# A two-block transformer kernel: how the first norm's scales arrive, who clears the queries, how many projection pieces run ahead of the first scores, and four zero products fewer ahead of attention 2

## The chip, the cores and the metric

The kernel runs on one core of one Trainium2 chip. The metric is the device time of one execution in microseconds; the figure of a kernel is the median of several runs.

## The reference, cut to what matters

The kernel computes two transformer blocks in float32 over 256 tokens of width 1024. Only the first steps of block 1 and the entry of block 2 matter here.

```
# block 1
h    = x * rsqrt(mean(x*x) + 1e-6) * attn_pre_g             # (256, 1024)
proj = h @ w_in                                             # (1024, 2304)
q_a, k_a, v_a, q_b, k_b, v_b = split(proj)                  # 512, 128, 128, 512, 512, 512
y_a  = sliding window attention with sinks (8 heads), then RMS norm
y_b  = differential attention (4 heads, two maps each), then RMS norm per head
x    = x + rms_norm(concat(y_a, y_b) @ w_out, attn_post_g)
x    = x + rms_norm(conv_ffn(rms_norm(x, ffn_pre_g)), ffn_post_g)
# block 2: adaptive norm of x by c, w_in_2, stick-breaking and dilated attention, w_out_2,
# then 32 experts with two-level routing; every expert's weights are read
```

## The kernel before, in words

TensorE (PE) multiplies, ScalarE (ACT) and VectorE (DVE) prepare operands and empty its banks, GpSimd (POOL) builds constants and takes inverse roots, SyncE (SP) issues the weight loads. Each engine runs its own list in written order and waits on semaphores; the order around the change is written out by hand.

**Weights and products.** Weights come in chunks of 2 MB into a ring of three places (chunk 0 in two halves). Most products are made of three: ACT rounds a half chunk to a short float (`split_one`, L1529), DVE subtracts to get the rest (`split_one`, L1871), and PE multiplies high by high, high by rest, rest by high (`product`, L903 to L905). The activations are split likewise: ACT's `rounded` (L1515) and DVE's `low` (L1852) read the turned tiles from the banks and scale them by a column of gains.

**Head of the kernel.** ACT issues 12 small loads into `stage` (rows of 128 values: taps of the convolution, c, and eight gain vectors, `attn_pre_g` among them) and then loads its table. SP issues x (two halves of 512 KB), the weight chunks, `swa_sinks` and the four lambda rows. DVE first clears the query tile `qz` (L2068, 128 x 4096), then takes the mean squares of both token tiles (L1818), POOL the roots (L783), and DVE scales both tiles (L2073). PE meanwhile makes 16 products of zeros (`stay_awake`, L874), turns token tile 0 (L892), makes four more products of zeros, waits for all 12 small loads, turns `stage` in three pieces (L1085 to L1087) and turns token tile 1. DVE copies the turned gains to `vec` (L2076 to L2078), and only then do ACT's `rounded`, DVE's first `split_one` and PE's first products (`project_first(4)`, L1103, L1110, L1125) go.

**Pieces.** The projection of block 1 is cut into 16 pieces (`items1`): 0 to 3 are queries of chunk 0; 4 (a key) and 5 (a value, 48 short products) are of chunk 1; 6 is a query of chunk 1; 7, 9, 10 and 11 are of chunk 2, 8 of chunk 1, 12 to 14 of chunk 3, 15 of chunk 4. A key or query piece is 24 products. `AHEAD = [6, 10]`: pieces 0 to 5 are made before attention 1, each in its own bank; the others are made between the units of attention (`BETWEEN`, L464). ACT empties even pieces, DVE odd ones (`take`).

**Attention 1** (L968) has 12 units. In step i PE makes scores i+1 (L978), turns the probabilities of unit i-1 (L1002), makes the value products of unit i-2 (L1016), and then the pieces of `BETWEEN[0][i]`. `scores(0)` waits until pieces 0 to 5 are taken. DVE's list ahead of its first softmax is: lambda, take pieces 1 and 3, split both halves of chunk 2, take piece 5, wait for the masks (`bias`, L816 and L818 on POOL).

**Ahead of attention 2** (L1228 to L1242) PE turns token tile 0 of the normed rows, sums the modulation's columns, turns the sums, makes five products of zeros (L1236), turns token tile 1, makes three more, and starts the products of the second projection.

**The experts** (from L1458) take 16 pairs; SP loads each matrix (2 MB) into one of ten places as soon as PE has read what lay in it (`pair_loads`, L679).

Of the kernel before, what the change touches and what calls it, by code (L numbers as in the profile page):

```python
# [19 lines left out]
def two_block_kernel(nc, a, out):  # L20
# [4 lines left out]
    ALU = mybir.AluOpType  # L25
# [5 lines left out]
    P = 128  # L31
# [3 lines left out]
    KD = D // P  # L35
# [40 lines left out]
    N_IN = 0  # L76
# [15 lines left out]
    with ctx:  # L92
# [11 lines left out]
        def sem(name):  # L104
            return ctx.enter_context(nc.semaphore(name))
# [3 lines left out]
        kT = sb("kT", [P, 8, S])  # L109
# [61 lines left out]
        hsq = cell(T, DIFF_H)  # L171
        frac = cell(NEXP)


# [78 lines left out]
        stage = kT[:, 0:2, :].rearrange("p k s -> p (k s)")[:, 0:384].rearrange("p (a b) -> p a b", a=3)  # L253

        PS = [ctx.enter_context(nc.psum_tensor(f"bank{i}", [P, HALF], f32)) for i in range(8)]

# [10 lines left out]
        s_rows = sem("s_rows")  # L267
        s_sink = sem("s_sink")
        s_lamv = sem("s_lamv")
# [184 lines left out]
        def item_waits(blk, n):  # L454
# [8 lines left out]
        AWAKE_AFTER = [{10: 2}, {}]  # L463
        BETWEEN = [{0: [6], 1: [7], 2: [8], 3: [9], 4: [10], 5: [11], 6: [12], 7: [13, 14], 8: [15]},  # L464
                   {0: [10, 11], 1: [12], 2: [13], 3: [14], 4: [15, 16], 5: [17], 6: [18], 7: [19]}]
# [134 lines left out]
        def _(sp):  # L600
# [29 lines left out]
            for c in range(1, LANES):  # L630
                straight(N_IN + c, w_in[:, :, c * HALF:(c + 1) * HALF])
            sp.dma_start(sinks, a["swa_sinks"][0].partition_broadcast(P)).then_inc(s_sink, 16)
            for n, name in enumerate(("diff_lq1", "diff_lk1", "diff_lq2", "diff_lk2")):
# [127 lines left out]
        def _(pool):  # L761
# [34 lines left out]
            pool.memset(ones[:, :], 1.0).then_inc(s_const, 1)  # L796
            pool.memset(zrow[:, :], 0.0).then_inc(s_const, 1)
            inverse_roots(T)
            then(pool.memset(from_here[:, :], 1.0))
# [70 lines left out]
        def _(pe):  # L870
            def stay_awake(bank, count):

                for _ in range(count):
                    pe.matmul(bank[:, :], zrow[:, 0:P], zrow[:, :], start=True, stop=True)  # L874
# [204 lines left out]
            pe.wait_ge(s_const, 3)  # L1079
            stay_awake(PS[7], 16)  # L1080
            turn("attn1", hn, range(T - 1))

            stay_awake(PS[6], 4)
            pe.wait_ge(s_stage, 16 * 12)
            pe.transpose(PS[7][:, 0:P], stage[:, 0, :], ident[:, :])  # L1085
            pe.transpose(PS[7][:, P:2 * P], stage[:, 1, :], ident[:, :])
            pe.transpose(PS[7][:, 2 * P:2 * P + 53], stage[0:53, 2, :], ident[0:53, 0:53]).then_inc(s_vecT, 1)  # L1087
            turn("attn1", hn, range(T - 1, T))
            pe.wait_ge(s_vec, 1)

            def project_first(count):
# [31 lines left out]
                for n in range(count):  # L1123
# [3 lines left out]
                    last.then_inc(s_gemm[0], 1)  # L1127

            project_first(4)
            for n in range(4, AHEAD[0]):  # L1130
                project(0, N_IN, n)
# [102 lines left out]
            for n in range(2):  # L1234
                turn_column_sums(n)
            stay_awake(PS[6], 5)  # L1236
            turn("attn2", rows2, range(T - 1, T))
# [240 lines left out]
        def _(sc):  # L1478
# [8 lines left out]
            cw = a["conv_w"].rearrange("o j (f p) -> (o j f) p", p=P)  # L1487
            cb = a["conv_b"].rearrange("o (f p) -> (o f) p", p=P)
            sc.dma_start(stage[:, 0, :], cw[0:P, :]).then_inc(s_stage, 16)
            sc.dma_start(stage[0:FT, 1, :], cw[P:P + FT, :]).then_inc(s_stage, 16)  # L1490
# [131 lines left out]
            sc.wait_ge(s_vec, 1)  # L1622
            rounded("attn1", lambda k: vec[:, 2, R_PRE + k:R_PRE + k + 1])
            split_one(N_IN, 1)
# [3 lines left out]
            sc.activation(lam2, lam2, ACT.Exp).then_inc(s_lame, 1)  # L1628
            take(0, range(AHEAD[0]))
            softmaxes(0, BETWEEN[0], SPLITS[0])  # L1630
# [159 lines left out]
        def _(ve):  # L1790
# [276 lines left out]

            ve.memset(qz[:, :, :], 0.0).then_inc(s_qzero, 1)  # L2068
            for t in range(T):
# [5 lines left out]
            ve.wait_ge(s_vecT, 1)  # L2075
            ve.tensor_copy(vec[:, 0:2, :], PS[7][:, 0:2 * P].rearrange("p (a b) -> p a b", a=2))  # L2076
            then(ve.tensor_copy(vec[:, 2, 0:53], PS[7][:, 2 * P:2 * P + 53]))
            ve.tensor_scalar(subc, vec[:, 2, R_SUB:R_SUB + 1], 1.0 - LAMBDA_INIT, None, ALU.mult).then_inc(s_vec, 1)  # L2078
            split_one(N_IN, 0)
            low("attn1", lambda k: vec[:, 2, R_PRE + k:R_PRE + k + 1])  # L2080
            split_one(N_IN, 1)
            split(N_IN + 1)

            ve.wait_ge(s_lamv, 64)
# [4 lines left out]
            ve.wait_ge(s_sink, 16)  # L2089
# [371 lines left out]
```

## Time and profile before

| | us |
|---|---|
| median of 3 runs | 1016.91 |
| the three runs | 1016.75, 1016.91, 1019.25 |
| the profiled execution's own time | 1018.49 |
| its span | 1016.8 |

The span runs from the first to the last instruction of the profiled execution; its own time holds 1.7 us more around it. Times in the profile are microseconds from the span's start. Busy time is counted per engine; "idle before" is how long an engine sat idle before an instruction, with what released it. The granted clock is 1.00 at 2.4 GHz and 0.50 at 1.2 GHz.

### The profile page before, as it was taken

Reading aid. Unit: us, or ns where it says so; the run is one execution under the profiler, and the core shown is the slowest. Engines: PE = TensorE matmul, PEld = TensorE weight load, DVE = VectorE, ACT = ScalarE, POOL = GpSimd, SP = SyncE. Lnnn points to the kernel's source line nnn. Section 1 sums busy time; section 2 is a strip of 40 time slices with the busy share of each in tenths; the row PEclk is TensorE's granted clock in tenths of the full one; section 3 lists DMA queues with packets and bytes.
Section 4 is the critical chain, followed back from the end, with each engine's and each line's share of the span. In section 5 each row is a group of like instructions: output and inputs, shape, how many; then the busy total and the mean of one; then the engine's idle time right before and its main releaser. Section 6 shows DMA issues by size and latency. Waiting matters only on the chain.

```text
span 1016.8 us, 15438 instructions
## 1 busy us (share of the span) xinstructions
PE 987.2 (97%) x5970; PEld 688.3 (68%) x5970; DVE 550.7 (54%) x1043; ACT 344.2 (34%) x574; POOL 81.8 (8%) x118
## 2 busy tenths in 40 slices
PE   8899999999999998999999999999999999999997
PEld 6898799999999997889865444444444444443342
DVE  7557689899989998839435422222222222222222
ACT  5555664545445555446341211111111111110112
POOL 7300110111111200200002000000000000000000
PEclk9999999999999999999999999999999999999999
DMA  8334176798879754354747899999999999999993
GB/s 301 125 125 166 66 258 228 275 337 298 310 281 351 285 203 165 131 202 166 305 191 258 329 365 424 414 431 425 428 427 429 429 426 429 427 429 427 429 422 160
DMA packets 60006, 312.15 MB, mean 307 GB/s; under 512 B 4117, under 2 KB 5498, under 8 KB 47418
## 3 DMA queue, kind: packets, MB, share of 16 engines
q1 hardware_dynamic: 52160, 284.83, 70.0%
q0 software_dynamic: 7392, 26.54, 7.3%
q8 instruction: 32, 0.52, 0.2%
q10 hardware_dynamic: 410, 0.16, 0.1%
q14 instruction: 12, 0.10, 0.0%
HBM read 310.47 MB, written 1.05 MB: 306 GB/s over the span
## 4 chain that ended last, share of the span: by engine, by line
PE 86%; DMA 6%; DVE 5%; ACT 2%; issue 1%; POOL 1%; SPq 0%; DVEq 0%; ACTq 0%
PE bank L903 12%; PE bank L904 12%; PE bank L905 12%; PE bank L1423 10%; PE bank L1451 10%; PE bank L1407 9%; PE bank L1351 6%; DMA eslots<-in_w_up 4%; PE bank L1050 3%; PE bank L1368 3%; DMA ring<-in_w_in 2%; PE bank L978 1%; PE bank L1016 1%; DVE ring_r L1871 1%; ACT ring_r L1529 1%
## 5 line engine op out<-in xcount | busy, mean ns | idle before, releaser
L903 PE MATMUL bank<-hT_r,ring_r 128*128 128x256 f32 x664 | 190.0, 286 | 1.1 <-DVE ring_r L1871 1.1
L905 PE MATMUL bank<-hT_r,ring_r 128*128 128x256 f32 x664 | 188.5, 284 | 0.0
L1871 DVE TENSOR_TENSOR ring_r<-ring,ring_r 128x2048 fp32r<-128x2048 f32 (+1 forms) x74 | 164.5, 2258 | 11.4 <-ACT ring_r L1529 11.0
L1529 ACT ACTIVATE ring_r<-ring 128x2048 fp32r<-128x2048 f32 (+1 forms) x74 | 136.6, 1889 | 40.1 <-DMA ring<-in_w_up 34.8
L904 PE MATMUL bank<-v_tok_r,ring_r 128*128 128x256 f32 x496 | 140.5, 283 | 0.0
L903 PEld LDWEIGHTS bank<-hT_r,ring_r 128*128 128x128 f32 x664 | 128.1, 193 | 1.9 <-DVE ring_r L1871 1.3
L905 PEld LDWEIGHTS bank<-hT_r,ring_r 128*128 128x128 f32 x664 | 128.0, 193 | 0.0
L1423 PE MATMUL bank<-eslots,scratch 128*64 128x512 f32 x512 | 114.5, 600 | 5.3 <-issue 3.0
L1451 PE MATMUL bank<-eslots,scratch 128*64 128x512 f32 x496 | 113.4, 596 | 0.7 <-ACT scratch L1761 0.7
L1407 PE MATMUL bank<-eslots,scratch 128*64 128x512 f32 x512 | 112.7, 593 | 0.0
L2352 DVE TENSOR_TENSOR scratch<-scratch,bank 128x512 f32<-128x512 f32 x16 | 11.0, 687 | 158.8 <-PE bank L1423 158.8
L904 PEld LDWEIGHTS bank<-v_tok_r,ring_r 128*128 128x128 f32 x496 | 95.3, 192 | 0.2
L1423 PEld LDWEIGHTS bank<-eslots,scratch 128*64 128x64 f32 x512 | 38.7, 139 | 79.1 <-issue 76.2
L905 PE MATMUL bank<-ring_r,hn_r 128*128 128x512 f32 (+2 forms) x240 | 88.3, 368 | 0.0
L1407 PEld LDWEIGHTS bank<-eslots,scratch 128*64 128x64 f32 x512 | 37.2, 137 | 72.2 <-issue 72.0
L1451 PEld LDWEIGHTS bank<-eslots,scratch 128*64 128x64 f32 x496 | 35.7, 137 | 62.8 <-issue 61.9
L2364 DVE SCALAR_TENSOR_TENSOR scratch<-bank,scratch,post_ffn 128x512 f32<-128x512 f32 x32 | 22.6, 746 | 99.7 <-PE bank L1451 99.7
L1765 ACT ACTIVATE scratch_r<-scratch 128x512 fp32r<-128x512 f32 x32 | 20.2, 631 | 148.3 <-DVE scratch L2364 147.9
L1351 PEld LDWEIGHTS bank<-scratch,hn 128*128 128x128 f32 x512 | 58.4, 192 | 12.7 <-issue 12.2
L783 POOL TENSOR_TENSOR small<-small 128x1 f32<-128x1 f32 (+1 forms) x20 | 15.1, 758 | 634.3 <-DVE small L2425 455.2
L1749 ACT ACTIVATE scratch<-bank,small 128x128 f32<-128x128 f32 x64 | 18.2, 368 | 135.3 <-PE bank L1351 135.3
L1351 PE MATMUL bank<-scratch,hn 128*128 128x128 f32 x512 | 61.4, 279 | 0.0
(308 smaller groups left out, 1449.7 us busy)
## 6 DMA issues: line engine op xcount, KB each, us to landing
eslots<-in_w_gate SPq DMA_DIRECT2D x31, 2048.0 KB, 25.7
eslots<-in_w_up SPq DMA_DIRECT2D x30, 2048.0 KB, 20.1
eslots<-in_w_down SPq DMA_DIRECT2D x28, 2048.0 KB, 24.3
ring<-in_w_up SPq DMA_DIRECT2D x16, 2048.0 KB, 11.7
ring<-in_w_in SPq DMA_DIRECT2D x9, 2048.0 KB, 7.9
ring<-in_w_down SPq DMA_DIRECT2D x8, 2048.0 KB, 9.1
kT<-in_w_ada POOLq DMA_DIRECT2D x24, 512.0 KB, 7.7
ring<-in_w_out SPq DMA_DIRECT2D x4, 2048.0 KB, 8.1
```

The lines of the kernel that those rows point to most:

```text
L903: pe.matmul(dst, lhs[0], rhs[0], start=start, stop=False, **flags)
L904: pe.matmul(dst, lhs[0], rhs[1], start=False, stop=False, **flags)
L905: return pe.matmul(dst, lhs[1], rhs[0], start=False, stop=stop, **flags)
L1050: last = pe.matmul(PS[PROJ_BANKS[1][t, c]][:, :], hT[:, k, t * P:(t + 1) * P], w[:, k % HALF_K, c * HALF:(c + 1) * HALF], start=(first and ...
L1351: last = pe.matmul(XB[k // 4][:, (k % 4) * P:(k % 4 + 1) * P], hn[:, t, k * P:(k + 1) * P], oneh[:, t, :], start=(t == 0), stop=(t == T - 1))
L1368: last = pe.matmul(ACC[2 * t + c][:, :], combT[:, t, :], ye[:, part, c * HALF:(c + 1) * HALF], start=False, stop=False, skip_group_check=True)
L1407: last = pe.matmul(GB[64 * e:64 * e + 64, :], xeT[:, k, 64 * e:64 * e + 64], weights(0, e, k), start=(k == 0), stop=(k == KD - 1))
L1423: last = pe.matmul(UB[64 * e:64 * e + 64, :], xeT[:, k, 64 * e:64 * e + 64], weights(1, e, k), start=(k == 0), stop=(k == KD - 1))
L1451: last = pe.matmul(XB[c][64 * e:64 * e + 64, :], eactT[:, f, 64 * e:64 * e + 64], weights(2, e, f)[:, c * HALF:(c + 1) * HALF], start=(f = ...
L1529: sc.activation(hi, raw, ACT.Copy).then_inc(s_whi, 1)
L1871: last = ve.tensor_tensor(lo, raw, hi, ALU.subtract)
L2364: ve.scalar_tensor_tensor(ye_sum[:, half], PS[4 + c][:, :], wslot, post_ffn[:, half], ALU.mult, ALU.mult).then_inc(s_yg, 1)
```

## The change

Six edits in the first part of block 1 and one ahead of attention 2.

- `attn_pre_g` is also loaded by a small load of its own (8 rows of 128), as the first that ACT issues. PE turns it into bank 5 after 12 of now 18 products of zeros, waiting for `s_pre`; DVE copies it to `pre_gain` (128 x 8), and `rounded` and `low` of the first norm read this.
- The three turns of `stage` move behind `project_first(4)` (`turn_gains`, bank 2), DVE's copies of them behind its split of chunk 1.
- `qz` is cleared by POOL, after `zrow` and ahead of the two roots, and not by DVE.
- Piece 6 is made before attention 1, after a wait for the take of piece 2, whose bank it uses; each later piece moves one step forward in `BETWEEN[0]`. ACT takes piece 6 ahead of its softmaxes. What `scores(0)` waits for is as before (pieces 0 to 5).
- DVE takes piece 5 between the two halves of the split of chunk 2, and not behind both.
- `swa_sinks` counts on the semaphore of the lambda rows, and four products of zeros between the turns of the two token tiles become three.
- Ahead of attention 2 five products of zeros become one.

```diff
-        BETWEEN = [{0: [6], 1: [7], 2: [8], 3: [9], 4: [10], 5: [11], 6: [12], 7: [13, 14], 8: [15]},
+        BETWEEN = [{0: [7], 1: [8], 2: [9], 3: [10], 4: [11], 5: [12], 6: [13], 7: [14], 8: [15]},
@@ gpsimd
             pool.memset(zrow[:, :], 0.0).then_inc(s_const, 1)
+            pool.memset(qz[:, :, :], 0.0).then_inc(s_qzero, 1)
             inverse_roots(T)
@@ tensor
-            stay_awake(PS[7], 16)
+            stay_awake(PS[7], 12)
+            pe.wait_ge(s_pre, 16)
+            pe.transpose(PS[5][:, 0:KD], pre_rows, ident[0:KD, 0:KD]).then_inc(s_vecT, 1)
+            stay_awake(PS[7], 6)
             turn("attn1", hn, range(T - 1))
-            stay_awake(PS[6], 4)
-            pe.wait_ge(s_stage, 16 * 12)
-            (three turns of stage)
+            stay_awake(PS[6], 3)
             turn("attn1", hn, range(T - 1, T))
...
             project_first(4)
-            for n in range(4, AHEAD[0]):
+            turn_gains()
+            for n in range(4, AHEAD[0] + 1):
+                if n == AHEAD[0]:
+                    pe.wait_ge(s_evA[0], 2)
                 project(0, N_IN, n)
             attention(0, N_IN, BETWEEN[0])
...
-            stay_awake(PS[6], 5)
+            stay_awake(PS[6], 1)
             turn("attn2", rows2, range(T - 1, T))
@@ scalar
+            sc.dma_start(pre_rows, a["attn_pre_g"].rearrange("o (f p) -> (o f) p", p=P)).then_inc(s_pre, 16)
             sc.dma_start(stage[:, 0, :], cw[0:P, :]).then_inc(s_stage, 16)
...
-            take(0, range(AHEAD[0]))
+            take(0, range(AHEAD[0] + 1))
+            sc.wait_ge(s_vec, 2)
@@ vector
-            ve.memset(qz[:, :, :], 0.0).then_inc(s_qzero, 1)
...
             ve.wait_ge(s_vecT, 1)
-            (copies of the turned stage, subc)
+            ve.tensor_copy(pre_gain, PS[5][:, 0:KD]).then_inc(s_vec, 1)
+            ve.wait_ge(s_vec, 1)
             split_one(N_IN, 0)
             low("attn1", ...)
             split_one(N_IN, 1)
             split(N_IN + 1)
+            ve.wait_ge(s_vecT, 2)
+            (copies of the turned stage, subc)
...
             take(0, range(AHEAD[0] - 2))
-            split(N_IN + 2)
+            split_one(N_IN + 2, 0)
             take(0, range(AHEAD[0] - 2, AHEAD[0]))
+            split_one(N_IN + 2, 1)
             ve.wait_ge(s_mask, 1)
```

## Rows read from the trace of the kernel before

**Rows 1.** The page: busy time, share of the span and instructions of each engine.

```profile
PE 987.2 (97%) x5970; PEld 688.3 (68%) x5970; DVE 550.7 (54%) x1043; ACT 344.2 (34%) x574; POOL 81.8 (8%) x118
```

**Rows 2.** Stretches: us, busy us (instructions) per engine, granted clock (PEclk), DMA share, GB/s.

```profile
32.50:35.10 2.60, 0.03 (x1) 0.02 (x1) 2.44 (x2) 0.00 (x0) 1.64 (x3) 1.00 0.08 33
37.00:38.00 1.00, 1.00 (x7) 1.00 (x6) 0.85 (x9) 0.40 (x3) 0.00 (x0) 0.50 0.83 270
```

**Rows 3.** Timeline, PE, 24 to 62: start, us, engine, line, operation [idle before <- releaser].

```profile
24.17 0.28 PE L903 MATMUL bank<-hT_r,ring_r 128*128 128x256 f32 x1
32.25 0.28 PE L905 MATMUL bank<-ring_r,hn_r 128*128 128x128 f32 x1
35.12 2.56 PE L978 MATMUL bank<-kT,scratch 128*128 128x128 f32 x16 [2.59 <-DVE v_tok L1887]
41.38 1.03 PE L978 MATMUL bank<-kT,scratch 128*128 128x256 f32 x4
60.78 1.06 PE L978 MATMUL bank<-kT,scratch 128*128 128x128 f32 x8
```

**Rows 4.** Timeline, DVE, 0 to 36, same columns.

```profile
1.85 3.47 DVE L2068 MEMSET scratch<- 128x4096 f32 x1 [1.85 <-PEq L2450]
7.99 1.58 DVE L2073 TENSOR_SCALAR hn<-x_tok,small 128x1024 f32<-128x1024 f32 x2 [0.44 <-POOL small L783]
17.20 6.68 DVE L1871 TENSOR_TENSOR ring_r<-ring,ring_r 128x2048 fp32r<-128x2048 f32 x3
29.82 4.69 DVE L1871 TENSOR_TENSOR ring_r<-ring,ring_r 128x2048 fp32r<-128x2048 f32 x2
34.55 0.42 DVE L1887 COPY v_tok<-bank 128x256 f32<-128x256 f32 x1
```

**Rows 5.** Timeline, PE, before 13.

```profile
2.37 5.26 PE L874 MATMUL bank<-zrow 128*128 128x512 bf16 x16 [2.37 <-POOL zrow L797]
8.80 1.10 PE L892 MATMUL bank<-ident,hn 128*128 128x128 f32 x8 [1.17 <-DVE hn L2073]
12.59 4.06 PE L1103 MATMUL bank<-hT_r,ring_r 128*128 128x256 f32 x32 [0.40 <-ACT hT_r L1515]
```

**Rows 6.** Timeline, ACT, 9 to 40.

```profile
9.37 1.91 ACT L1529 ACTIVATE ring_r<-ring 128x2048 fp32r<-128x2048 f32 x1 [1.71 <-DMA ring<-in_w_in]
11.97 3.03 ACT L1515 ACTIVATE hT_r<-bank,vec 128x256 fp32r<-128x256 f32 x8 [0.69 <-PE bank L892]
17.39 3.72 ACT L1529 ACTIVATE ring_r<-ring 128x2048 fp32r<-128x2048 f32 x2 [0.58 <-DMA ring<-in_w_in]
27.67 1.54 ACT L1541 ACTIVATE scratch<-bank 64x256 f32<-64x256 f32 x4
38.77 0.39 ACT L1562 ACTIVATE scratch<-scratch,small 128x128 f32<-128x128 f32 x1
```

**Rows 7.** Issue of x on SP, and swa_sinks: time from issue to landing.

```profile
DMA to landing us min/median/max: 3.7/4.3/4.8
...
small<-in_swa_sinks SPq DMA_DIRECT2D x1, 4.0 KB, 15.9
```

**Rows 8.** GpSimd by line, min/median/max ns: roots (0 to 12), a later memset, bias rows.

```profile
L783 POOL TENSOR_TENSOR small<-small x2: 842/1150/1459, 6.5 to 7.9; 128x1 f32<-128x1 f32 x2
...
L852 POOL MEMSET scratch<- x1: 3519/3519/3519, 415.3 to 415.3; 128x4096 f32 x1
...
L816 POOL TENSOR_SCALAR bias<-post_attn x8: 848/850/7007, 11.9 to 26.5; 128x256 f32<-128x256 f32 x8
```

**Rows 9.** Timeline, PE and DVE, ahead of attention 2.

```profile
413.09 1.24 PE L874 MATMUL bank<-zrow 128*128 128x512 bf16 x5
...
412.31 0.75 DVE L1824 TENSOR_SCALAR kT<-x_tok,small 128x1024 f32<-128x1024 f32 x1 [0.66 <-POOL small L783]
```

**Rows 10.** A stretch of the expert stage, and what SP's loads waited for (us, times, longest).

```profile
920.00:940.00 20.00, 17.93 (x92) 6.83 (x88) 4.99 (x13) 1.86 (x3) 0.00 (x0) 1.00 1.00 428
...
SPq L670 <- PE bank L1451: 157.5, 13, 12.5
```

More of the change, by code:

```diff
@@ L172, in two_block_kernel @@
         frac = cell(NEXP)
+        pre_gain = frac[:, 0:KD]
         qz = scratch[:, 0:4096].rearrange("p (h s) -> p h s", s=S)
@@ L253, in two_block_kernel @@
         stage = kT[:, 0:2, :].rearrange("p k s -> p (k s)")[:, 0:384].rearrange("p (a b) -> p a b", a=3)
+        pre_rows = kT[0:KD, 2, 0:P]
         PS = [ctx.enter_context(nc.psum_tensor(f"bank{i}", [P, HALF], f32)) for i in range(8)]
@@ L267, in two_block_kernel @@
         s_rows = sem("s_rows")
-        s_sink = sem("s_sink")
+        s_pre = sem("s_pre")
         s_lamv = sem("s_lamv")
@@ L631, in _ @@
                 straight(N_IN + c, w_in[:, :, c * HALF:(c + 1) * HALF])
-            sp.dma_start(sinks, a["swa_sinks"][0].partition_broadcast(P)).then_inc(s_sink, 16)
+            sp.dma_start(sinks, a["swa_sinks"][0].partition_broadcast(P)).then_inc(s_lamv, 16)
             for n, name in enumerate(("diff_lq1", "diff_lk1", "diff_lq2", "diff_lk2")):
@@ L1079, in _, with turn_gains @@
             pe.wait_ge(s_const, 3)
-            stay_awake(PS[7], 16)
+            stay_awake(PS[7], 12)
+            pe.wait_ge(s_pre, 16)
+            pe.transpose(PS[5][:, 0:KD], pre_rows, ident[0:KD, 0:KD]).then_inc(s_vecT, 1)
+            stay_awake(PS[7], 6)
             turn("attn1", hn, range(T - 1))
-            stay_awake(PS[6], 4)
-            pe.wait_ge(s_stage, 16 * 12)
-            pe.transpose(PS[7][:, 0:P], stage[:, 0, :], ident[:, :])
-            pe.transpose(PS[7][:, P:2 * P], stage[:, 1, :], ident[:, :])
-            pe.transpose(PS[7][:, 2 * P:2 * P + 53], stage[0:53, 2, :], ident[0:53, 0:53]).then_inc(s_vecT, 1)
-            turn("attn1", hn, range(T - 1, T))
-            pe.wait_ge(s_vec, 1)
+            stay_awake(PS[6], 3)
+            turn("attn1", hn, range(T - 1, T))
+            def turn_gains():
+                pe.wait_ge(s_stage, 16 * 12)
+                pe.wait_ge(s_hT["attn1"], KD)
+                pe.transpose(PS[2][:, 0:P], stage[:, 0, :], ident[:, :])
+                pe.transpose(PS[2][:, P:2 * P], stage[:, 1, :], ident[:, :])
+                pe.transpose(PS[2][:, 2 * P:2 * P + 53], stage[0:53, 2, :], ident[0:53, 0:53]).then_inc(s_vecT, 1)
             def project_first(count):
@@ L1127, in project_first @@
                     last.then_inc(s_gemm[0], 1)
+            pe.wait_ge(s_vec, 1)
             project_first(4)
-            for n in range(4, AHEAD[0]):
+            turn_gains()
+            for n in range(4, AHEAD[0] + 1):
+                if n == AHEAD[0]:
+                    pe.wait_ge(s_evA[0], 2)
                 project(0, N_IN, n)
@@ L1622, in _ @@
             sc.wait_ge(s_vec, 1)
-            rounded("attn1", lambda k: vec[:, 2, R_PRE + k:R_PRE + k + 1])
+            rounded("attn1", lambda k: pre_gain[:, k:k + 1])
             split_one(N_IN, 1)
@@ L2075, in _ @@
             ve.wait_ge(s_vecT, 1)
-            ve.tensor_copy(vec[:, 0:2, :], PS[7][:, 0:2 * P].rearrange("p (a b) -> p a b", a=2))
-            then(ve.tensor_copy(vec[:, 2, 0:53], PS[7][:, 2 * P:2 * P + 53]))
-            ve.tensor_scalar(subc, vec[:, 2, R_SUB:R_SUB + 1], 1.0 - LAMBDA_INIT, None, ALU.mult).then_inc(s_vec, 1)
+            ve.tensor_copy(pre_gain, PS[5][:, 0:KD]).then_inc(s_vec, 1)
+            ve.wait_ge(s_vec, 1)
             split_one(N_IN, 0)
-            low("attn1", lambda k: vec[:, 2, R_PRE + k:R_PRE + k + 1])
+            low("attn1", lambda k: pre_gain[:, k:k + 1])
             split_one(N_IN, 1)
             split(N_IN + 1)
-            ve.wait_ge(s_lamv, 64)
+            ve.wait_ge(s_vecT, 2)
+            ve.tensor_copy(vec[:, 0:2, :], PS[2][:, 0:2 * P].rearrange("p (a b) -> p a b", a=2))
+            then(ve.tensor_copy(vec[:, 2, 0:53], PS[2][:, 2 * P:2 * P + 53]))
+            ve.tensor_scalar(subc, vec[:, 2, R_SUB:R_SUB + 1], 1.0 - LAMBDA_INIT, None, ALU.mult).then_inc(s_vec, 1)
+            ve.wait_ge(s_lamv, 80)
             for n in range(2):
@@ L2088, in _ @@
             last.then_inc(s_lamx, 1)
-            ve.wait_ge(s_sink, 16)
             ve.tensor_scalar(negsink, sinks, -1.0, None, ALU.mult)
```

## The prediction, written before the change was run

> **What bounds the kernel now.** I read the page first: PE is busy 97% of the span [rows 1], so the kernel is as long as PE's list, and what can be won is an idle stretch of PE, a stretch at a low clock, or work that PE need not do. The waits of PE over the first 100 us name one long stop, 2.6 us before the first scores of attention 1. In PE's timeline the last product of piece 5 starts at 32.25 and `scores(0)` starts at 35.12, released by DVE's copy of piece 5 [rows 3]. DVE's timeline shows why: it splits both halves of chunk 2 from 29.82 for 4.69 us and only then copies the piece, at 34.55 [rows 4]. The stretches around it show the second price: PE does nothing from 32.5 to 35.1, and from 37 to 38 its granted clock is 0.50, the level of 1.2 GHz, while the clock was 1.00 in the gap itself [rows 2]. So sixteen score products and piece 6 take from 35.12 to 41.38, 6.26 us [rows 3].
>
> The head is a chain: x lands, mean squares, roots, DVE scales the tiles [rows 4], PE turns them from 8.80 [rows 5], ACT rounds from 11.97, and the first product follows at 12.59 [rows 5, 6]. ACT had split its first half chunk by 11.28 (9.37 + 1.91) and then waited 0.69 us [rows 6], for gains that come only after all 12 small loads.
>
> **The change, part by part.**
>
> *Gains alone.* ACT can round from 11.3 and not 11.97, and DVE can start its first split as much earlier. The turn of tile 1 must be there by then. DVE's scaling of both tiles ends at 9.57 (7.99 + 1.58) [rows 4]; PE then has tile 0 from 8.8 to 9.9 and three zero products, at 0.2 us each, to 10.5, and needs 0.3 us for the first turns of tile 1. So the first product starts at about 11.9, 0.67 earlier. From there to piece 4 PE needed 11.58 us (12.59 to 24.17) [rows 3, 5]: 23.5. The three turns of `stage`, now here, cost 0.14 us each (1.10 us for 8) [rows 5]: 23.9. But piece 4 also waits for chunk 1, which ACT can split only when it has landed, from 17.39 for 3.72 us [rows 6]; DVE follows with 2.23 us a half (6.68 for 3) [rows 4]: 19.3, 21.5, 23.8. Before it was 23.88. So piece 4 starts at 23.96 in place of 24.17. Of 0.67 us the transfer of chunk 1 leaves **0.2 us**. Bounds: 0.3 if the turns fit beside the wait, and a loss of 0.4 if the head is not early at all and the turns come on top.
>
> *The wait for the gains' own load* stands in PE's list with the turn of tile 0 behind it. Twelve zero products end near 6.6; six more and the turn end near 8.1, ahead of the 8.8 at which tile 0 is there [rows 5]. The load's landing is not in the trace. By the nearest rows it is between 3.7 us after its issue (x, issued at the same 0.93, so 4.6) and 15.9 us (`swa_sinks`, issued into a full queue, so 16.8) [rows 7]. I take the first end: the queues are empty then. The issue adds 0.4 us to ACT's list, which sits idle 1.71 us before its first split [rows 6].
>
> *Queries cleared by POOL.* DVE loses 3.47 us at 1.85 [rows 4]. Its end at 5.32 released the first mean square; x landed at about 4.6 and 6.2 (0.93 + 3.7, 1.38 + 4.8) [rows 7], so the second mean square, which follows the second tile, gains 0.1 at most. POOL pays 3.52 us, the time of the same clearing in block 2 [rows 8], from 2.3 to 5.8, and its first root is not asked for before 6. But the two engines disturb each other: a bias row that takes 0.85 us took 7.01 us while DVE split chunks, and a root beside the second mean square took 1.46 us [rows 8]. If the clearing is held in the same way by both mean squares (from 4.9 to 7.5), it ends at 8.3 and the first root at 8.8 in place of 8.0; tile 0 is turned from 9.7, the first product starts at 12.5, and piece 4 at 24.5. Cost 0.5 us. Against it: in block 2 the clearing took 3.52 us with DVE's subtractions of two SBUF operands beside it, which is no more than DVE's own 3.47 [rows 4, 8]. I take no hold, and keep 0.5 for the range.
>
> The page "SBUF — State Buffer" of the Trainium skill (two separate sides) says that a DVE operation with two SBUF inputs blocks only a GpSimd operation that reads SBUF. The long bias row and the long root agree with it, and a clearing reads nothing. By that rule the 0.5 us are not due; without it the sum would be 4.9 and not 5.4.
>
> *Piece 5 taken between the halves; piece 6 ahead of the scores.* From piece 4 on PE now has: pieces 4 and 5 as before, 24.17 to 32.36, 8.19 us; piece 6, 24 products at 0.12 us, 2.88 us; sixteen score products at full clock, twice 0.88 us (the eight at 60.78 [rows 3] end with the next operation's start), 1.76 us. Sum 12.83. Before, the same work took 41.38 - 24.17 = 17.21 us [rows 3]. Gain **4.4 us**, of which 2.6 is the stop and 1.8 the low clock.
> Is the cover there? DVE starts its half at 29.82, ends it at 32.1, copies piece 5 when PE has it (32.2 to 32.8) and ends the second half at 35.1 [rows 4]; PE is on piece 6 until 35.0. `scores(0)` then waits for nothing. Piece 7, of chunk 2, starts at 36.8, 1.7 us after its split. Piece 6's wait for the take of piece 2 is met at 29.2 (four copies from 27.67 in 1.54 us) [rows 6]. Next in line are the turns of unit 0: its fourth exponential ended 4.0 us after the scores began (39.16 - 35.12) [rows 3, 6]; PE comes to it after 1.76 + 2.88 + 0.88 = 5.5 us. Margin 1.5 us. The masks of POOL ended at 32.8; DVE needs them at 36.
> Behind this the list holds the same work, one piece further on, up to piece 14; there it stands as before. The takes of pieces 12 and 13 now precede the last splits of chunk 4 by one step, which still leaves over 2 us. I cost the reordering at 0; bounds -1 to +1, since a POOL root beside a DVE split can go either way.
>
> *Four zero products fewer.* Five took 1.08 us of PE's pace (1.24 with the last one's end), 0.215 each; the rows of tile 1 are ready at 413.06 [rows 9], before the first of them has run. So PE turns tile 1 **0.86 us** sooner, ACT's rounding follows the turn, and the products follow that. Bounds: 0.86, and a loss of 1.4 if the clock falls (below).
>
> *The rest.* Everything later hangs on PE. In the expert stage DMA is busy all the time and PE loses 2.1 us in 20 [rows 10], but every load is released by PE's reading of a place (SP's waits [rows 10]), so a shift of PE shifts the stream. I cost it at 0.
>
> Sum: 0.2 + 4.4 + 0.86 = 5.4 us. The profiled execution's own time was 1018.49 (span 1016.8 and 1.7 around it), 1.6 above the median of the runs; the shift is the same on both: 1016.91 - 5.4 = **1011.5**, and a profile of the new kernel would have a span near 1011.4.
>
> **Rivals.**
>
> *A: the clock falls ahead of attention 2.* PE does less there. In attention 1 a low clock cost PE about half of some 4.5 us [rows 2]. For: the zero products stand there for it. Against: they are followed and preceded by turns without a gap, and the low clock in attention 1 came after 2.6 us of nothing. Price: 2.3 lost of the gain: 1013.8.
>
> *B: the gain is taken back inside attention 1.* Softmax work that was covered by two pieces in step 7 now has one. For: PE did stop after that, between 82 and 97. Against: both pieces stand ahead of the same point. Price 2 us: 1013.5.
>
> *C: the expert stage has its own end.* If the stream of weights, busy all the time [rows 10], were bound to its first load and not to PE, all would be given back: 1016.9. Against: SP's waits.
>
> *D, the slower one: the gains' load lands late.* Place: PE's wait ahead of tile 0. If it took the 15.9 us of `swa_sinks` [rows 7], it would land at 16.8; six zero products and the turn of tile 0 end at 19.3, tile 1 at 21, the first product starts at 21.5, 8.9 late, for a result of 1016.9 + 8.9 - 5.2 = 1020.6. It costs something from a landing after 7.5, and makes the kernel slower from about 13. Against: all 12 small loads, the last issued at 6.1, had landed by 10.5.
>
> That the change does not do what it says is the case in which DVE's half of chunk 2 still delays the copy; it would take a later start of that half, and nothing moves it.
>
> **How the numbers follow.** Forecast 74% (own range 1010.3 to 1012.8: 0.5 for the clearing, 1 for the reordering), A 7%, B 10%, C 5%, D 4%. The three runs before spread over 2.5 us, which can lift a median. Range: 1009.8 to 1014.2, which takes in A and B. A measurement of this kernel can tell 0.3%, 3.05 us, from no change: faster means under 1013.86. The forecast, A and B lie under it, the last two barely; with the spread of the runs I give faster 0.85, same 0.10, slower 0.05.
>
> **What would show it.** PE: first product at 11.9, piece 4 at 24.0, no gap between piece 6 and `scores(0)`, which starts near 35.0, and clock 1.00 from 30 to 42. DVE: copy of piece 5 near 32.4. POOL: a clearing of 3.5 us from 2.3. ACT: rounding from 11.3. One zero product ahead of tile 1 in block 2. Wrong would be: a first product after 12.6, a gap of PE in 35 to 42, a clock of 0.50 near 37 or 411, or a stop between 75 and 100 that grows by over a microsecond.

## The result and the profile after

The changed kernel takes **1013.53 us** (median of 8 runs, 1012.39 to 1014.09); the kernel before, run beside it on the same chip, takes 1018.82 (8 runs, 1016.75 to 1020.18). The ratio is 0.9944 with an interval of 0.9931 to 0.9957: 5.3 us faster by the medians, where 5.4 was forecast, and the whole interval lies beyond the 0.3% that the prediction asked for. The absolute time lies 2.0 above the forecast, because it was hung on a median of three runs (1016.91) that was itself 1.9 low.

The profiled execution of the new kernel took 1013.88 us, with a span of 1012.2 (before: 1018.49, span 1016.8; forecast for the span: near 1011.4). PE is still the whole kernel:

```profile
PE 986.6 (97%) x5968; PEld 687.1 (68%) x5968; DVE 547.4 (54%) x1043; ACT 343.9 (34%) x574; POOL 81.5 (8%) x119
```

Its busy time fell by only 0.6 us against [rows 1], while the span fell by 4.6.

**Ahead of attention 1.** The stretches around the old stop, in the changed kernel (us; busy us and count of PE, PEld, DVE, ACT, POOL; granted clock; DMA share; GB/s), answer to [rows 2]:

```profile
30.00:32.50 2.50, 2.50 (x25) 2.50 (x24) 2.03 (x1) 0.68 (x2) 0.99 (x2) 1.00 0.72 277
32.50:35.00 2.50, 2.50 (x23) 2.50 (x23) 2.27 (x2) 0.00 (x0) 0.00 (x0) 1.00 0.80 270
35.00:37.00 2.00, 2.00 (x20) 2.00 (x19) 0.69 (x4) 0.76 (x2) 0.00 (x0) 1.00 0.00 0
37.00:39.00 2.00, 2.00 (x19) 2.00 (x18) 1.97 (x17) 1.07 (x5) 0.00 (x0) 1.00 0.00 0
```

PE is busy in all of it and the granted clock is 1.00, so it ran at the level of 2.4 GHz throughout. PE's timeline answers to [rows 3]:

```profile
24.24 0.39 PE L907 MATMUL bank<-hT_r,ring_r 128*128 128x256 f32 x1
...
35.46 1.95 PE L982 MATMUL bank<-kT,scratch 128*128 128x128 f32 x16
...
40.12 1.03 PE L982 MATMUL bank<-kT,scratch 128*128 128x256 f32 x4
```

`scores(0)` waits for nothing. It starts 0.34 later than before, but with piece 6 made, and the next scores at 40.12 come with piece 7 made too, which before was made after them. DVE's timeline shows what let it through, against [rows 4]: the copy of piece 5 at 32.73, between the two halves of chunk 2.

```profile
19.49 4.69 DVE L1888 TENSOR_TENSOR ring_r<-ring,ring_r 128x2048 fp32r<-128x2048 f32 x2 [0.49 <-ACT ring_r L1545]
...
29.74 2.29 DVE L1888 TENSOR_TENSOR ring_r<-ring,ring_r 128x2048 fp32r<-128x2048 f32 x1
32.73 0.42 DVE L1904 COPY v_tok<-bank 128x256 f32<-128x256 f32 x1 [0.70 <-PE bank L909]
33.07 2.28 DVE L1888 TENSOR_TENSOR ring_r<-ring,ring_r 128x2048 fp32r<-128x2048 f32 x1
```

**The head.** Four rows of its timelines (PE, POOL, DVE, ACT in this order) answer to [rows 4 to 6]:

```profile
11.97 1.07 PE L1114 MATMUL bank<-hT_r,ring_r 128*128 128x256 f32 x7
...
2.27 3.50 POOL L801 MEMSET scratch<- 128x4096 f32 x1
...
4.74 1.22 DVE L1835 CUSTOM_DVE_ANT_0 mix<-x_tok 128x1024 f32<-128x1024 f32 x1 [4.74 <-DMA x_tok<-in_x]
...
11.36 3.03 ACT L1531 ACTIVATE hT_r<-bank,small 128x256 fp32r<-128x256 f32 x8
```

The gains are no longer awaited, the first product comes 0.62 earlier, and piece 4 comes at 24.24, which is not earlier at all. Over all the profiles of this study piece 4 starts at 24.12 to 24.90 with the new head (8 profiles, two of them with the queries cleared another way) and at 24.17 to 24.62 with the old one (6).

**Ahead of attention 2**, one zero product stands ahead of tile 1, against [rows 9]:

```profile
411.69 0.38 PE L878 MATMUL bank<-zrow 128*128 128x512 bf16 x1
411.91 1.04 PE L896 MATMUL bank<-ident,kT 128*128 128x128 f32 x8
...
413.24 0.47 PE L962 MATMUL bank<-hT_r,ring_r 128*128 128x256 f32 x1
```

From the first turn of block 2 (406.31) to these products it is 6.93 us; before it was 7.80 (407.70 to 415.50). That is 0.87.

**Where the 4.6 us of the spans lie.** I took the start of the same instruction in both profiles at five points and subtracted. The last column is a second profile of the changed kernel, from the third set of runs:

```
stretch                                        forecast  profile  second profile
start to piece 4                                 -0.2     +0.07      +0.73
piece 4 to the first residual update (121.4)     -4.4     -4.19      -4.20
from there to the first turn of block 2           0       +2.73      +0.14
that turn to the products of block 2             -0.86    -0.87      -0.87
from there to the end                             0       -2.34      -2.20
sum (spans 1012.2 and 1010.4)                    -5.4     -4.6       -6.4
```

The two steps that the change makes directly repeat within 0.01 us. Everything else in the table moves by up to 2.6 us between two executions of one program, and that is what the experiments had to separate.

### The profile page after: what moved, and what is told of

It is laid out like the page before. It is cut to its first block, busy times and chain, and to the rows that moved or that the text cites. A ratio compares the mean times of both kernels' runs of the same rounds, so it can differ in the third digit from the quotient of the medians.

```text
span 1012.2 us, 15440 instructions
## 1 busy us (share of the span) xinstructions
PE 986.6 (97%) x5968; PEld 687.1 (68%) x5968; DVE 547.4 (54%) x1043; ACT 343.9 (34%) x574; POOL 81.5 (8%) x119
## 4 chain that ended last, share of the span: by engine, by line
PE 74%; DVE 10%; DMA 8%; issue 4%; ACT 2%; POOL 1%; DVEq 0%; SPq 0%; ACTq 0%
PE bank L1466 10%; PE bank L1438 10%; PE bank L1422 10%; PE bank L907 8%; PE bank L908 8%; PE bank L909 8%; PE bank L1366 6%; DMA eslots<-in_w_up 4%; DVE ring_r L1888 3%; DMA ring<-in_w_up 3%; PE bank L1054 3%; PE bank L1383 3%; DVE scratch L2151 1%; DMA ring<-in_w_in 1%; PE bank L982 1%
```

## The experiments

Each comparison is with the kernel before, run on the same chip in the same set of runs. In the first set before took 1018.28 (27 runs), in the second 1018.66 (18), in the third 1018.38 (11). "Shift" below is the start of an instruction in the profile against the same one in the profile before.

### One part of the change at a time

**Taking piece 5 between the halves, alone.**

```
             take(0, range(AHEAD[0] - 2))
-            split(N_IN + 2)
+            split_one(N_IN + 2, 0)
             take(0, range(AHEAD[0] - 2, AHEAD[0]))
+            split_one(N_IN + 2, 1)
```

> The kernel before with one edit: DVE takes piece 5 between the two halves of its split of chunk 2. Theory (each of the two edits alone opens the way): the copy of piece 5 runs as soon as PE has made it, 32.6 to 33.0, and the first scores start at 33.1 and not at 35.1. The gap is 0.7 us, the clock stays at 1.00, scores(2) starts at 37.7 and not 41.4; gain 3.7 us. Rival (only both edits together help, since the second half of the split is then late for piece 7 or the clock falls all the same): gain under 2 us.

Measured: 1014.54 (6 runs, 1013.6 to 1015.27), ratio 0.9954 (0.9939 to 0.9969), span 1013.2. PE stopped for 0.61 us only:

```profile
33.39 0.79 PE L978 MATMUL bank<-kT,scratch 128*128 128x128 f32 x5 [0.61 <-DVE v_tok L1887]
```

The shift is -3.25 at the next scores (`scores(2)`) and -3.23 at the first residual update: the stop less 0.6, and the low clock gone. By the median it is 3.7, as expected.

**One more piece ahead of the first scores, alone** (the list of pieces between the units moved by one, `range(4, AHEAD[0] + 1)` with its wait, ACT's take of seven pieces).

> The kernel before with one edit: piece 6 is made ahead of the first scores, DVE's order stays (both halves of chunk 2, then piece 5). Theory: PE makes piece 6 from 32.4 to 35.2 while DVE splits, the copy of piece 5 ends at 35.0, the first scores start at 35.2 at full clock and scores(2) follows piece 7 at 39.9; gain 4.4 us, no less than with both edits. Rival: the copy comes later than before, since DVE is the bound, and the gain is under 3 us.

Measured: 1015.67 (10 runs, 1014.08 to 1016.87), ratio 0.9971 (0.9956 to 0.9987), span 1013.5. The shift is -4.08 at the first residual update. So piece 6 alone covers the stop, since PE reaches `scores(0)` at 35.54, after DVE has taken piece 5 (34.20 and 0.42 us). By the median the gain is 2.6 and not the 4.4 expected; in the profile 1.3 us of the shift were lost again by the first turn of block 2, with a fall of the clock near 392.

**Both, without head and zeros.** Run in the third set, to see whether the two add.

> The kernel before with the two edits of the attention part together (piece 6 ahead of the scores, piece 5 taken between the halves), head and zero products as before. Theory (each alone removes the stop; together they add nothing to piece 6 alone): scores(0) at 35.4, scores(2) at 40.1 with piece 7 made, 4.1 to 4.4 us ahead of before at the first normed residual; median 1014 to 1015. Rival (the head's edits carry a part of the whole): 0.5 us or more slower than the changed kernel beyond the 0.86 us of its zero products.

Measured: 1013.91 (5 runs, 1012.92 to 1014.39), ratio 0.9954 (0.9939 to 0.9968), span 1012.2; shift -4.00 at the first residual update. Locally it is no more than piece 6 alone. The two edits buy much the same time, and with both the margin is wider: DVE starts the copy at 32.88 and not at 34.20. The changed kernel, run in the same set, took 1013.06 and so 0.85 us less, which is what its four zero products give in the trace (0.86) and leaves nothing for the head, as far as runs that spread over 1.5 to 2 us can tell.

**The head alone** (gains' own load, clearing by POOL, the late turns of `stage`).

> The changed kernel with the projection order, DVE's order of piece 5 and the zero products ahead of attention 2 as before; left are the gains loaded alone, the turns of the staged rows behind the first pieces, and the queries cleared by GpSimd. Theory (the transfer of chunk 1 takes the head's lead away, and chunk 2's split the rest): first product 0.6 us earlier, piece 4 at 24.0 to 24.3 as before, first scores at 35.1, granted clock 0.50 behind it, total within 0.5 us of before. Rival (the lead of the head reaches the end): 0.6 us faster or more.

Measured: 1017.12 (10 runs, 1015.63 to 1018.58), ratio 0.9983 (0.997 to 0.9996), span 1015.2. The first product starts at 11.82, 0.77 earlier; piece 4 at 24.16, with a shift of -0.01. The median is 1.2 us lower nevertheless, by which the rival (0.6 us or more) would have been right. No row of the profile accounts for that.

**The four zero products alone.**

> The kernel before with one edit: one product of zeros and not five ahead of the second turn in block 2. Theory: the products of the second projection start 0.86 us sooner after the first turn there, clock 1.00. Rival (the clock falls): the next 64 products take 0.24 us each in place of 0.12 for some time, and the kernel is slower by about 1.4 us.

Measured: 1018.19 (10 runs, 1016.76 to 1020.16), ratio 1.0 (0.9988 to 1.0012), span 1015.1. From the first turn to the products of block 2 it is 6.94 us in place of 7.80: the 0.86 is in the trace. The median doesn't show it, and this profile has a low clock at 390 that the profile before has not.

What these five say together: the gain is in the attention part, 4 us, and 0.86 us in the zero products; by the traces piece 6 alone gets all of the 4 us and the other edit 3.2.

### What the low clock behind a stop costs

My forecast charged 1.8 us of low clock to the stop of 2.6 us, as a fixed price. Two profiles above, in which neither edit of the attention part was made, say otherwise. First zeros alone, then the head alone, from the stop on:

```profile
32.30:34.80 2.50, 0.77 (x7) 0.63 (x6) 2.36 (x2) 0.00 (x0) 0.00 (x0) 1.00 0.95 300
34.80:37.00 2.20, 2.16 (x19) 2.19 (x20) 0.88 (x7) 0.00 (x0) 0.00 (x0) 1.00 0.10 32
37.00:39.00 2.00, 2.00 (x19) 2.00 (x19) 1.55 (x13) 1.68 (x9) 0.00 (x0) 1.00 0.00 0
```

```profile
32.30:34.80 2.50, 0.30 (x3) 0.17 (x3) 2.34 (x2) 0.00 (x0) 0.00 (x0) 0.74 0.44 161
34.80:37.00 2.20, 2.18 (x10) 2.20 (x11) 0.00 (x0) 0.00 (x0) 0.00 (x0) 0.50 0.03 7
37.00:39.00 2.00, 2.00 (x11) 2.00 (x10) 1.56 (x11) 0.71 (x4) 0.00 (x0) 0.50 0.00 0
39.00:41.00 2.00, 2.00 (x14) 2.00 (x13) 0.96 (x7) 2.00 (x13) 0.00 (x0) 0.67 0.00 0
```

The granted clock stayed at 1.00 in the one; in the other it fell within the stop and was 0.50, the level of 1.2 GHz, for all of 34.8 to 39. The stops were not quite the same: PE stood still for 1.77 us ahead of `scores(0)` with zeros alone, for 2.22 with the head alone and for 2.59 in the kernel before. From `scores(0)` to the next scores it is 4.74 us (34.84 to 39.58), 7.29 (34.82 to 42.11) and, before, 6.26 (35.12 to 41.38). So the low clock cost 0, 2.5 and 1.5 us in three executions; I had read one of them.

To take the stop and the clock apart I let PE multiply zeros while it waits, in the kernel before:

```
+            pe.wait_ge(s_hT["attn1"], KD)
+            stay_awake(PS[3], 11)
             attention(0, N_IN, BETWEEN[0])
```

> The kernel before with eleven products of zeros put in the stop of PE ahead of the first scores; nothing else. They separate the stop from the clock. Theory (the stop costs its 2.6 us always, the clock behind it falls in some executions only): scores(0) still starts at 35.1 and scores(2) at 39.7 in this profile; the median falls by 0.5 to 1.3 us against before and the spread of the runs shrinks from about 5 us towards 3. Rival (the fall of the clock is a fixed cost of 1.6 us as in the first profile): 1.6 us in every run.

Measured: 1017.76 (10 runs, 1014.58 to 1019.1), ratio 0.9987 (0.9975 to 0.9999), span 1015.0. `scores(0)` starts at 35.01 and the next scores at 39.75, 4.74 us later: the wait for DVE stays, the clock doesn't fall, and the shift at the first residual update is -1.63. Set beside -4.00 with both attention edits, the remainder, 2.4, is the stop. By the median 0.9 us arrived, within the 0.5 to 1.3 expected, but the interval (0.1 to 2.5 us) holds the rival's 1.6 too, and the runs spread over 4.5 us and not over 3. What speaks against the rival is zeros alone, where the clock didn't fall without any filling. In this run's own profile the 1.63 were lost again before block 2: the shift is +0.38 at its first turn, at a granted clock of 1.00, after 1.4 us of waits of PE for DVE's splits.

**A second stop of the same length.** In every profile so far PE waits 2.6 us for DVE near 393, ahead of the last `down` of block 1. Here is the kernel before, and then the changed one, where the clock falls behind it:

```profile
393.30:396.20 2.90, 0.43 (x2) 0.00 (x1) 1.23 (x1) 2.38 (x2) 0.00 (x0) 1.00 0.27 83
396.20:398.50 2.30, 2.21 (x10) 1.85 (x11) 1.78 (x1) 2.29 (x2) 0.00 (x0) 1.00 1.05 408
```

```profile
390.33:393.00 2.67, 0.39 (x2) 0.00 (x0) 1.54 (x2) 2.18 (x2) 0.00 (x0) 1.00 0.39 75
393.00:395.00 2.00, 1.72 (x6) 1.43 (x7) 1.42 (x2) 2.00 (x2) 0.00 (x0) 0.76 1.03 396
395.00:397.00 2.00, 2.00 (x6) 1.55 (x5) 2.00 (x2) 0.47 (x1) 0.00 (x0) 0.50 1.04 401
```

The clock was 1.00 before the stop in both. The fall costs 1.6 us in the changed kernel (its shift goes from -3.01 before the stop to -1.39 at the first turn of block 2), and it is the largest part of the +2.73 in the table. Over the profiles of this study in which the stop stands as it was, the clock fell behind it in 5 of 11 (the changed kernel, piece 6 alone, both attention edits, zeros alone, the queries cleared by DVE). Across the stop the shift moves by 1.4 to 1.6 us in these five and by less than 0.05 in the other six; in its second profile the changed kernel has the stop and no fall.

I filled this stop with zeros in the changed kernel:

```
+            pe.wait_ge(s_conv, 4 * CHUNKS)
+            stay_awake(PS[0], 10)
             down(CHUNKS - 1, seq_down(CHUNKS - 1), bank_done=s_bank)
```

> The changed kernel with ten products of zeros in the stop of 2.7 us ahead of the last down projection (PE waits there for DVE's rest of the last activations, at 390). Theory (a stop of this length lets the clock fall in some executions, as in the changed kernel's profile, 1.6 us, and in three of six profiles so far): the products behind the stop take 0.23 us each from the first on, the turn of block 2 starts 0.7 us sooner on average; median 0.3 to 1.0 us under the changed kernel. Rival (zero products end after DVE is ready and cost as much as they save): same or slower.

Measured: 1013.24 (6 runs, 1010.89 to 1013.69), ratio 0.9939 (0.9924 to 0.9955), span 1011.6, no fall near 390; the shift stays at -3.8 from 380 to the first turn of block 2. The changed kernel wasn't run in this set. Against before the ratios are 0.9939 here and 0.9944 and 0.9948 for the changed kernel, so the medians don't show the 0.3 to 1.0 us that I expected. That the zeros keep the clock isn't proven either: it stayed at 1.00 in all three profiles with this stop filled (this one and two below), but so it did in six of the eleven without.

**The changed kernel again**, an identical program, as the measure of what differs between executions and sets.

> The changed kernel once more, unchanged, for a second profile. Theory (the fall of the clock behind a stop of over 2 us comes in some executions only): the head, the scores and the first normed residual within 0.4 us of the first profile; the products behind the stop at 390 at 0.23 us a piece or at 0.43, as it comes; median 1013 to 1014. Rival (this kernel's timing fixes where the clock falls): the fall at 390 as in the first profile, and none between 920 and 970.

Measured: 1013.06 (5 runs, 1012.06 to 1013.99), ratio 0.9948 (0.9933 to 0.9963), span 1010.4. The median is as expected, and the fall at 390 did not come again, against the rival; between 920 and 970 there was none again, as the rival had it. The head, the scores and the first residual update came 0.56, 0.66 and 0.65 us later than in the first profile, not within 0.4.

### The clearing of the queries

Two runs weigh the 0.5 us that I kept for engines disturbing each other. Clearing by DVE as before, in the changed kernel:

> The changed kernel with the queries cleared by DVE again, ahead of the mean squares. Theory (chunk 1 hides the head): first mean square at 5.3 in place of 4.7, second at 6.4 in place of 6.1, first product at most 0.3 us later, piece 4 within 0.1 us; total the same as the changed kernel. Rival (the clearing on GpSimd is worth its 0.6 us): 0.5 us slower or more.

Measured: 1014.41 (5 runs, 1012.71 to 1014.88), ratio 0.9953 (0.9938 to 0.9969), span 1012.7. The mean squares start at 5.24 and 6.32, as expected; the first product at 12.46 and piece 4 at 24.81 are later than the 0.3 and 0.1 us allowed. But ACT could begin with the weights only at 10.05 here, as at 10.11 in the second profile of the changed kernel, and that has 12.53 and 24.90 with the clearing on POOL. So the lateness is that of the weights, and the trace shows no price of clearing on DVE. The medians can't tell: the ratio is 0.9953 against 0.9944 and 0.9948, and the intervals overlap.

Clearing by POOL with an operation that reads SBUF:

```
-            pool.memset(qz[:, :, :], 0.0).then_inc(s_qzero, 1)
+            pool.wait_ge(s_const, 3)
+            pool.tensor_copy(qz[:, :, :], zrow[:, 0:S].unsqueeze(1).broadcast_to([P, 16, S])).then_inc(s_qzero, 1)
```

> The changed kernel with GpSimd's clearing of the queries made as a copy of a row of zeros, so that it reads SBUF as well as writes it. It tells apart whether DVE's mean squares (two SBUF inputs) hold up only GpSimd's readers. Theory (they do): the copy, some 4 us alone, is stretched by the mean squares to 7 to 8.5, the roots come 1 to 1.5 us late and the first product 0.5 to 1.5 us late. Rival (what was free is the place, not the kind of operation): the copy takes 4 us and ends near 6.5 beside the first mean square, roots on time.

Measured: 1012.63 (3 runs, 1012.52 to 1015.1), ratio 0.9946 (0.9928 to 0.9964), span 1010.9. Its timelines of POOL and DVE:

```profile
2.38 3.60 POOL L802 CAST scratch<-zrow 128x4096 f32<-128x4096 bf16 x1
...
4.28 2.78 DVE L1836 CUSTOM_DVE_ANT_0 mix<-x_tok 128x1024 f32<-128x1024 f32 x1 [4.28 <-DMA x_tok<-in_x]
```

I had expected POOL's copy to be stretched. It took 3.60 us, and it was DVE's mean square that was held: 2.78 us in place of 1.22, until a microsecond after the copy's end. Beside the plain clearing (2.27 to 5.77) the same mean square took 1.22. So of these two readers the one that started first went on, and the clearing, which reads nothing, held nobody. The page "SBUF — State Buffer" of the Trainium skill (SBUF: two separate sides), weighed in the prediction, says both: a DVE operation with two SBUF inputs counts only against a GpSimd operation that reads SBUF, and of such a pair whichever starts first keeps the port for its whole length. This trace agrees, 3.60 us for the copy and 2.78 for the mean square. The delay reached the first root (7.15 in place of 6.05), hardly the first product (12.13 in place of 11.97, where 0.5 to 1.5 us were expected), and not piece 4 (24.22), which waits for chunk 1.

### The second stop filled with work, and zeros in the expert stage

The zeros in the stop near 390 do no work. Eight of the 12 products of the first bank of that `down` need only the high half of ACT's output; what the stop waits for is DVE's rest. So PE can start them early:

```
+                if bank_done is not None:
+                    pe.wait_ge(s_conv, 4 * CHUNKS)
+                    stay_awake(PS[0], 5)
+                    pe.wait_ge(s_ahi, i + 1)
...
+                            for k in range(KE):
+                                for part in range(2):
+                                    pe.matmul(PS[4][:, :], act_r[:, 0, k, 0:P], both(w, k, 0, HALF)[part],
+                                              start=False, stop=False, skip_group_check=True)
+                            pe.wait_ge(s_act, i + 1)
```

> The changed kernel with the stop at 390 shortened and filled: five products of zeros, then the eight products of the first bank that need only ACT's rounded activations, before the wait for DVE's rest. Theory: DVE's 1.23 us (its subtraction) leave the path, PE's stop falls from 2.6 us of nothing to under 1, and the clock does not fall; the turn of block 2 comes 1.2 us sooner than without, 1.9 on average with the clock; median 1011.5 to 1012.5. Rival (what follows waits for DVE's split of the next weights, not for PE): 0.5 us or less.

Measured: **1011.82** (6 runs, 1010.1 to 1013.03), ratio 0.9931 (0.9917 to 0.9945), span 1011.2. PE in the old stop:

```profile
389.35 1.25 PE L878 MATMUL bank<-zrow 128*128 128x512 bf16 x5
390.71 2.11 PE L1206 MATMUL bank<-ring_r,hn_r 128*128 128x512 f32 x8
392.66 1.07 PE L1210 MATMUL bank<-ring_r,hn_r 128*128 128x512 f32 x4
```

The shift goes from -4.22 ahead of the stop to -5.26 at the first turn of block 2, 1.0 us. On the same chip the changed kernel took 1013.06, so this is 1.2 us less; the intervals of the two ratios overlap, so by the medians the step is likely and not certain. The rival's 0.5 us is too little for the trace.

Zeros in the expert stage too:

```
+                if (u in (2, 3, 4) and r is not None) or last_one:
+                    pe.wait_ge(s_combT, p + 1)
+                    stay_awake(UB, 10)
```

> As high_first, with ten products of zeros ahead of the wait for the up weights in pairs 7 to 9, 12 to 14 and in the last pair, where PE stops for 2.1 us and the clock fell in nine of ten profiles. Theory (this part is bound by the transfers, 428 GB/s): the zero products cost nothing, and the clock stays; up to 1 us faster than high_first. Rival (PE is bound there and every product of zeros is paid, or places come free later): 2 to 10 us slower.

Measured: 1013.96 (6 runs, 1012.39 to 1015.8), ratio 0.9957 (0.9942 to 0.9972), span 1011.0. It is 2.1 us more than without the zeros, the least that the rival named.

But the edit doesn't do what I meant it to. Inside the loop the pairs are called with `u` from 5 to 9, so `u in (2, 3, 4)` never holds there, and only the last pair got its zeros: the trace has 96 products of zeros against 86 without the edit. The stop near 924 stands unfilled, 2.06 us, and the clock falls behind it at 924.6 as in the other profiles. In the last pair there was no stop to fill. First without the zeros, then with them:

```profile
976.87 7.04 PE L1438 MATMUL bank<-eslots,scratch 128*64 128x512 f32 x32
983.74 7.04 PE L1454 MATMUL bank<-eslots,scratch 128*64 128x512 f32 x32
```

```profile
974.21 7.04 PE L1438 MATMUL bank<-eslots,scratch 128*64 128x512 f32 x32
981.18 2.33 PE L878 MATMUL bank<-zrow 128*128 128x512 bf16 x10
983.44 7.09 PE L1457 MATMUL bank<-eslots,scratch 128*64 128x512 f32 x32
```

PE was 2.66 us ahead at the gate products and 0.30 ahead at the up products behind the zeros: the ten zeros took 2.4 us of PE's own time, and that is about the loss of the medians. (The span is no longer than without them, 1011.0 against 1011.2, because without them the clock fell behind the second stop of the stage; what that costs stands below.) Whether zeros in the real stops of this stage would pay was not measured.

## Why the prediction came out right

**The stop, 2.6 us: right.** It is gone, by the means forecast. Piece 6 alone is enough (shift -4.08), the copy between the halves alone leaves 0.6 of it (-3.23); both together give -4.00.

**The low clock, 1.8 us: near to right for the profile it was read from, where it was 1.5, and wrong as a fixed price.** The price behind this stop was 0, 1.5 and 2.5 us in three executions. The prediction treated one execution's reading as the kernel's. The table's -4.19 and -4.20 are against that one profile; against the one of zeros alone, where piece 4 came 0.45 us later, the stop was 1.77 us and the clock did not fall, the same stretch would have shown 1.9. Seen over many executions, the gain should be the stop plus a part of the low clock's price. The medians fit a part, without proving it: 3.7 us for the one edit, 2.6 for the other, 4.5 for both.

**The head, 0.2 us: the step failed, and cost nothing.** First product at 11.97 (forecast 11.9) and ACT's rounding at 11.36 (11.3) are right. Piece 4 came at 24.24 and not 23.96. The bound I named, chunk 1, is the right one: ACT split its first half from 17.54, DVE followed at 19.49 for 4.69, to 24.18. I had put DVE's two halves at 2.23 each from 19.3, without a gap behind ACT's first half, and got 23.8. In the second profile ACT began with its first half chunk only at 10.11, not 9.35, because the weights landed later, and piece 4 came at 24.90. The head is as early as its transfers, and these moved by 0.7 us between executions. What remains open is the 1.2 us by which the median of the head alone was lower; beside the attention edits, in the third set, the head added nothing.

**The gains' own load** (rival D): PE turned the gains at 7.60 behind its zeros, without a wait that the profile shows. D is out. The arithmetic of this step was off, though. The prediction had twelve zero products end near 6.6 and the last of the eighteen and the turn near 8.1. All twelve followed each other at 0.43 us here, where the kernel before went over to 0.22 from the ninth on, and the turn of tile 0 started at 9.35, though its rows were scaled at 8.00:

```profile
7.81 1.71 PE L878 MATMUL bank<-zrow 128*128 128x512 bf16 x6
9.35 1.04 PE L896 MATMUL bank<-ident,hn 128*128 128x128 f32 x8
```

It cost nothing only because ACT was busy with its first half chunk until 11.27, and that is luck. In the other profiles with this head the turn of tile 0 started at 8.39 to 9.45.

**Clearing by POOL: no hold, as taken.** 3.50 us against the forecast 3.5; mean squares of 1.22 and 1.23.

**Four zero products, 0.86 us: right** in the trace, three times 0.86 or 0.87. Rival A, the clock falling ahead of attention 2, did not occur there: the granted clock is 1.00 from 410 to 450. A fall did come 17 us earlier, behind a stop that was there before.

**Reordering, 0: right.** B is out: the shift is -4.12 at the first residual update and no stop between 75 and 100 grew. Behind it, in the loops of block 1, PE waited twice for DVE's splits in the profiled execution, 0.7 us in all, and the shift fell to -3.01 by 380. In the second profile it went from -3.47 to -3.30, so the change doesn't bring this about every time; why it came in the first is not shown.

```profile
PE bank L907 <- DVE hn_r L2186: 2.6, 1, 2.6
...
PE bank L907 <- DVE ring_r L1888: 0.7, 2, 0.5
```

**The expert stage, 0: the shift is carried on, but the number is wrong in each profile.** Rival C is out, since a shift of PE shifts the stream: at the issue of the up weights of the last pair but one (922.22 before) the shifts are -3.12 and -4.88. On top came 2.2 to 2.3 us between the products of block 2 and the end. 1.7 of these lie in one stretch that the profile before has and the two of the changed kernel have not:

```profile
960.50:965.00 4.50, 4.47 (x14) 1.76 (x16) 0.00 (x0) 0.00 (x0) 0.00 (x0) 0.62 1.01 430
```

PE is busy there at a clock of 0.62, behind a stop of over two microseconds. The fourteen profiles together show what this is worth. PE stops for 2.1 us near 930 in each. In seven the clock falls behind that stop; PE is then 1.7 us later at its next work, but the following stop, near 960, is 0.5 us in place of 2.2, so that the loss is given back. In five, the kernel before among them, it falls only behind the second stop, and nothing gives that back. In two, those of the changed kernel, it doesn't fall. From the issue at 922.22 to the end of the second stop's products the seven and the two gain 1.6 to 1.7 us on the profile before, and the other four gain nothing. So these 1.7 us come from where the clock fell in the profile before, and not from the change. The rest of the 2.2 to 2.3 is not explained.

So the sum was right partly because its errors cancel, and that is luck: against the forecast the profiled execution lost 0.3 us in the head, 0.2 around the stop, 1.1 and 1.6 later in block 1, and gained 2.3 behind it, for 4.6 in place of 5.4. The medians, 5.3 us apart, are the firmer evidence. What decides whether the clock falls behind a stop of 2.6 us is open. Before and after the stop the rows of executions with and without a fall look alike.

## What to carry to other kernels

Where PE waits for a copy queued behind a long operation of DVE, either put the copy between two parts of that operation or put independent products ahead of the wait. The two buy much the same time, so measure each alone before adding both. Price a stop at its idle time, and its low clock as a range, from nothing to as much again, until several executions have been read. Look whether a later stop gives a loss back. Products of zeros belong only where the trace shows PE standing still, and the trace must show afterwards that they ran there. An earlier start of the head is worth nothing when the next chunk's landing sets the pace.

## What the hardware showed unexpectedly

- The same stop of 2.6 us lowered the granted clock in some executions and not in others: behind the one near 390, in 5 of 11 profiles, for 1.4 to 1.6 us.
- A DVE mean square that began while POOL's copy was reading SBUF took 2.78 us in place of 1.22, and the copy was not stretched. In the kernel before it was POOL's bias row that took 7.01 us [rows 8]; it began at 17.58, when DVE's splits were running from 17.20 to 23.88, and ended 0.7 us behind them. In both cases the one that began later was held, for about as long as the other ran.
- Ten zero products in the stop near 390 cost nothing (a shift of -3.80 ahead of it, -3.84 behind it); ten in the last pair of the experts, where PE had no stop, cost 2.4 us of PE's time.
- In the expert stage a fall of the clock behind one stop, 1.7 us, was given back by the next stop; behind the last stop it was not.
